# Smaller token tiles in a 32-expert layer: 96 rows for 128, a bias selector built per item, and the output scaling and the down bias moved

## What is computed

```
logits = h @ w_router + b_router                  # [512, 32]
top_vals, top_idx = top_k(logits, 4); gate = softmax(top_vals)
for each expert e, on the tokens that chose it:
    gu = x @ w_gate_up[e] + b_gate_up[e]          # 1024 -> 2048
    g, u = min(gu[:, :1024], 7), clip(gu[:, 1024:], -7, 7)
    y = ((u + 1) * g * sigmoid(1.702 * g)) @ w_down[e] + b_down[e]
    out[token] += gate * y
```

## Time and profile before

| what | value |
|---|---|
| median of 3 executions | 1663.77 us (1662.95 to 1666.04) |
| profiled execution, its own time | 1666.04 us |
| span in its profile | 1664.3 us |
| PE busy | 1597.3 us (96%) |
| DVE busy | 1310.5 us (79%) |
| ACT busy | 1074.0 us (65%) |
| moved | 476.58 MB, 286 GB/s |

### The profile page before, as it was taken

How to read it: one execution, slowest core, us unless ns; L and a number is a source line. 1 busy time by engine, 2 the same in 40 slices (tenths; PEclk the granted TensorE clock), 3 DMA queues, 4 the chain that set the end, 5 groups by cost and what they waited for, 6 DMA issues and landing times.

```text
span 1664.3 us, 21630 instructions
## 1 busy us (share of the span) xinstructions
PE 1597.3 (96%) x7527; PEld 1266.9 (76%) x7527; DVE 1310.5 (79%) x1016; ACT 1074.0 (65%) x1113; POOL 145.5 (9%) x113
## 2 busy tenths in 40 slices
PE   7999899999969999999999999999999999999993
PEld 6788555678858888888888888888888888888882
DVE  4465464545579999998999999899999889999973
ACT  5243343422367777777777777777777777777762
POOL 6500000000010000010000001000000100000010
PEclk9999899999979999999999999999999999999997
DMA  8332000004489999999999999999999999999973
GB/s 289 120 102 76 16 1 1 1 26 177 149 343 357 381 380 381 380 373 356 381 380 381 380 380 368 362 380 381 379 383 381 360 367 382 379 381 382 378 250 126
DMA packets 114382, 476.58 MB, mean 286 GB/s; under 512 B 9704, under 2 KB 10224, under 8 KB 97872
## 3 DMA queue, kind: packets, MB, share of 16 engines
q1 hardware_dynamic: 100528, 432.83, 68.1%
q0 software_dynamic: 10224, 37.62, 8.8%
q10 hardware_dynamic: 3600, 5.73, 1.0%
HBM read 451.24 MB, written 24.90 MB: 286 GB/s over the span
## 4 chain that ended last, share of the span: by engine, by line
PE 94%; DVE 3%; DMA 1%; ACT 1%; issue 0%; ACTq 0%; SPq 0%; DVEq 0%; POOLq 0%
PE ps L1174 26%; PE ps L1176 26%; PE ps L1175 26%; PE ps L1429 3%; PE ps L1269 2%; PE ps L1245 2%; PE ps L1401 2%; PE ps L1409 2%; PE ps L1282 2%; PE ps L1249 1%; PE ps L1289 1%; DVE mx L898 1%; DVE split L839 1%; PE ps L1353 0%; DMA xs<-in_x 0%
## 5 line engine op out<-in xcount | busy, mean ns | idle before, releaser
L1036 DVE TENSOR_TENSOR chunk_lo<-chunk,chunk_hi 128x2048 fp32r<-128x2048 f32 x384 | 861.7, 2284 | 56.7 <-ACT chunk_hi L660 54.0
L660 ACT ACTIVATE chunk_hi<-chunk 128x2048 fp32r<-128x2048 f32 x378 | 722.9, 1914 | 136.5 <-PE ps L1176 135.5
L1174 PE MATMUL ps<-chunk_hi,XT 128*128 128x512 f32 x1024 | 413.7, 404 | 2.0 <-DVE XT L1081 2.0
L1176 PE MATMUL ps<-chunk_hi,XT 128*128 128x512 f32 x1024 | 401.1, 392 | 0.0
L1175 PE MATMUL ps<-chunk_lo,XT 128*128 128x512 f32 x1024 | 400.5, 391 | 0.0
L1174 PEld LDWEIGHTS ps<-chunk_hi,XT 128*128 128x128 f32 x1024 | 193.7, 189 | 42.7 <-DVE XT L1081 2.4
L1176 PEld LDWEIGHTS ps<-chunk_hi,XT 128*128 128x128 f32 x1024 | 192.6, 188 | 40.8
L1175 PEld LDWEIGHTS ps<-chunk_lo,XT 128*128 128x128 f32 x1024 | 193.1, 189 | 37.7
L1174 PE MATMUL ps<-chunk_hi,hidT 128*128 128x512 f32 x512 | 205.4, 401 | 1.6 <-DVE hidT L1088 1.6
L1176 PE MATMUL ps<-chunk_hi,hidT 128*128 128x512 f32 x512 | 199.8, 390 | 0.0
L1175 PE MATMUL ps<-chunk_lo,hidT 128*128 128x512 f32 x512 | 199.6, 390 | 0.0
(11 more groups left out here) (235 smaller groups left out, 1890.5 us busy)
## 6 DMA issues: line engine op xcount, KB each, us to landing
chunk<-in_w_gate_up SPq DMA_DIRECT2D x256, 1024.0 KB, 8.9
chunk<-in_w_down SPq DMA_DIRECT2D x128, 1024.0 KB, 6.1
raw<-in_w_in SPq DMA_DIRECT2D x14, 1024.0 KB, 7.6
w_out<-in_w_out SPq DMA_DIRECT2D x4, 1024.0 KB, 5.9
xs<-in_x SPq DMA_DIRECT2D x4, 512.0 KB, 5.1
raw<-in_w_branch_a SPq DMA_DIRECT2D x2, 1024.0 KB, 5.1
raw<-in_w_branch_b SPq DMA_DIRECT2D x2, 1024.0 KB, 4.9
sum_rows<-xs ACTq DMA_DIRECT2D x4, 512.0 KB, 2.6
```

The costliest lines, as they stand in the source:

```text
L660: a.activation(chunk_hi[hi_slot(c, nxt)][:, :], chunk[c][:, :], ACT.Copy).then_inc(ex_hi, 1)
L1036: v.tensor_tensor(chunk_lo[c][:, :], chunk[c][:, :], chunk_hi[hi_slot(c, nxt, first)][:, :].bitcast(F32), ALU.subtract).then_inc(ex_lo, 1)
L1174: mm(dst, lhsT(0), rhs(0), start=start, stop=False)
L1176: return mm(dst, lhsT(1), rhs(0), start=False, stop=stop)
```

## The change

- `CAP` goes from 128 to 96: the stationary operands `XT`, `hidT` and `onehot` are 96 columns wide, 96 rows are gathered, transposed (8 matmuls of 96 rows x 128 stationary columns against a 96x96 identity) and added; outputs are 96 rows. The table for `npass` now allows up to 6 passes.
- The fixed `pick` gives way to `sel` (96x96 bf16), which DVE fills for each item (`choose_bias`: one tensor_scalar compare of `part_mod` with a column of `erow`). PE's `add_bias` uses 96 partitions and no register. DVE waits for `down_begun` before it overwrites `sel`; PE waits for `sel_ready`.
- The down bias moves from behind the gate bias of i+1 to right behind the up bias of i; PE's wait for `y_ready` moves with it. The index result moves to bank 6, and the wait for `f5_ready` moves ahead of `hidden_T`.
- `rows_out(i)` moves from behind the second chunk split of item i+1 to the end of item i, ahead of those splits.
- In the last item DVE makes `chunk_lo` 8 behind the two operations on `hid` and no longer ahead of them.
- The bias table loses its 32 rows of zeros.

```diff
-CAP = 128
+CAP = 96
-        part_mod = sb("part_mod", [128, E])
-        pick = sb("pick", [128, E], BF16)
+        part_mod = sb("part_mod", [128, CAP])
+        sel = sb("sel", [96, CAP], BF16)
-        idx_ps = ps[0:CAP, 5, 448:453]
+        idx_ps = ps[0:CAP, 6, 448:453]
@@ gpsimd
-            g.memset(bias_new[96:128, :], 0.0).then_inc(part_mod_set, 1)
-            pool.wait_ge(part_mod_set, 4)
...
-            pool.dma_start(bias_parts, bias_new[:, :]).then_inc(scattered, 16)
+            pool.dma_start(bias_parts, bias_new[0:96, :]).then_inc(scattered, 16)
@@ scalar
-            def act_item(i, nxt, before=True):
+            def act_item(i, nxt):
                 if nxt:
-                    ex_split_hi(i + 1, 0)
-                    ex_split_hi(i + 1, 1)
-                if before:
-                    rows_out(i - 1, 12 * i + 6)
-                if nxt:
-                    ex_split_hi(i + 1, 2)
+                    for c in range(3):
+                        ex_split_hi(i + 1, c)
                     rows_hi(i + 2, 0)
...
                     ex_split_hi(i + 1, 7)
+                act.wait_ge(gates_set, i + 3)
+                a.activation(gate_c[:, :], gates[:, bass.ds(i % 4, 1)], ACT.Copy).then_inc(gate_ready, 1)
+                act.wait_ge(ex_used, order(i, 11, nxt) + 3)
+                act.wait_ge(gate_ready, i + 1)
+                act.wait_ge(scattered, 16 * i + ADDED)
+                a.activation(ysb, ps[0:CAP, 4:6, :].rearrange("p t n -> p (t n)"), ACT.Copy,
+                             scale=gate_c[:, 0:1]).then_inc(y_ready, 1)
@@ vector
+            def choose_bias(e):
+                v.tensor_scalar(sel[:, :], part_mod[0:96, :], erow[0:96, bass.ds(e, 1)], None,
+                                ALU.is_equal).then_inc(sel_ready, 1)
...
                     ex_split_lo(i + 1, 3)
-                else:
-                    ex_split_lo(i, 8, nxt)
...
                 if nxt:
+                    dve.wait_ge(down_begun, i + 1)
+                    choose_bias((i + 1) % E)
                     rows_lo(i + 2, 1)
-                    ex_split_lo(i, 8, nxt)
+                ex_split_lo(i, 8, nxt)
                 ex_split_lo(i, 9, nxt)
@@ tensor
-            def add_bias(e, bank, part, start):
+            def add_bias(bank, part, start):
                 for t in range(2):
                     col = part * FF + t * 512
-                    last = mm(ps[0:CAP, bank + t, :], pick[:, bass.ds(e, 1)].to_broadcast([128, CAP]),
-                              bias_tab[:, col:col + 512], start=start, stop=not start)
+                    last = mm(ps[0:CAP, bank + t, :], sel[:, :], bias_tab[0:96, col:col + 512], start=start, stop=not start)
...
-                add_bias(i % E, 2, 1, False).then_inc(up_ps, 1)
+                pe.wait_ge(sel_ready, i + 1)
+                add_bias(2, 1, False).then_inc(up_ps, 1)
+                pe.wait_ge(y_ready, i + 1)
+                add_bias(4, 2, True).then_inc(down_begun, 1)
...
                         if c == 0:
-                            pe.wait_ge(y_ready, i + 1)
                             slots(i + 3)
                         if c == 1:
+                            pe.wait_ge(f5_ready, i + 4)
                             pe.wait_ge(xt_lo, 2 * i + 4)
                             hidden_T(i + 1)
-                    add_bias((i + 1) % E, 0, 0, False).then_inc(gate_ps, 1)
-                    pe.wait_ge(f5_ready, i + 4)
+                    pe.wait_ge(sel_ready, i + 2)
+                    add_bias(0, 0, False).then_inc(gate_ps, 1)
                 else:
                     hidden_T(i + 1)
-                    pe.wait_ge(y_ready, i + 1)
-                add_bias(i % E, 4, 2, True)
                 pe.wait_ge(hidT_lo, i + 1)
```

More of the change, by code:

```diff
@@ L134, in encoder_block @@
         ex = shared[:, 128:256].rearrange("p (c e) -> p c e", e=E)
-        onehot = shared[:, 256:512].bitcast(BF16).rearrange("p (c n) -> p c n", n=CAP)
+        onehot = shared[:, 256:448].bitcast(BF16).rearrange("p (c n) -> p c n", n=CAP)
         gains = sb("gains", [128, 2, HD])
@@ L194, in encoder_block @@
         part_mod_set = sem("part_mod_set")
-        pick_set = sem("pick_set")
         gcol_ps = sem("gcol_ps")
@@ L260, in encoder_block @@
         xt_lo = sem("xt_lo")
+        sel_ready = sem("sel_ready")
         gate_ps = sem("gate_ps")
@@ L272, in encoder_block @@
         hidT_lo = sem("hidT_lo")
+        down_begun = sem("down_begun")
         y_ready = sem("y_ready")
@@ L363, in _ @@
             sp.wait_ge(scattered, ADDED)
-            sp.dma_start(bias_tab[:, :], bias_parts).then_inc(bias_back, 16)
+            sp.dma_start(bias_tab[0:96, :], bias_parts).then_inc(bias_back, 16)
             sp.wait_ge(gathered, 16)
@@ L440, in _ @@
             for q in range(3):
-                g.iota(part_mod[32 * q:32 * q + 32, :], pattern=[[0, E]], base=0, channel_multiplier=1,
+                g.iota(part_mod[32 * q:32 * q + 32, :], pattern=[[0, CAP]], base=0, channel_multiplier=1,
                        allow_small_or_imprecise_dtypes=True).then_inc(part_mod_set, 1)
                 pool.wait_ge(part_mod_set, q + 1)
-            g.memset(bias_new[96:128, :], 0.0).then_inc(part_mod_set, 1)
-            pool.wait_ge(part_mod_set, 4)
             pool.wait_ge(zero_set, 1)
@@ L755, in _ @@
             act.sem_inc(y_ready, 1)
[L757 to L765, removed]
-            def act_item(i, nxt, before=True):
-                if nxt:
-                    ex_split_hi(i + 1, 0)
-                    ex_split_hi(i + 1, 1)
-                if before:
-                    rows_out(i - 1, 12 * i + 6)
-                if nxt:
-                    ex_split_hi(i + 1, 2)
+            def act_item(i, nxt):
+                if nxt:
+                    for c in range(3):
+                        ex_split_hi(i + 1, c)
                     rows_hi(i + 2, 0)
@@ L795, in act_item @@
                     ex_split_hi(i + 1, 7)
-            act_item(0, True, False)
-            with act.Fori(1, last_item) as i:
+                act.wait_ge(gates_set, i + 3)
[5 more added lines that the diff above has]
+                             scale=gate_c[:, 0:1]).then_inc(y_ready, 1)
+            with act.Fori(0, last_item) as i:
                 act_item(i, True)
             act_item(last_item, False)
-            rows_out(last_item, order(last_item, 11, False) + 3)
             a.activation(warm[:, :], eps[:, :], ACT.Sqrt)
@@ L1100, in _ @@
             serve(1)
+            choose_bias(0)
             for c in range(1, 3):
@@ L1441, in _ @@
             pe.wait_ge(bias_back, 16)
-            pe.wait_ge(pick_set, 1)
-            add_bias(0, 0, 0, False).then_inc(gate_ps, 1)
+            pe.wait_ge(sel_ready, 1)
+            add_bias(0, 0, False).then_inc(gate_ps, 1)
             pe.wait_ge(items_ready, 1)
@@ L1516 @@
     args.append(nc.dram_tensor("sum_rows", (SEQ + CAP, D), f32, kind="Internal").ap())
-    args.append(nc.dram_tensor("bias_parts", (128, 3 * D), mybir.dt.bfloat16, kind="Internal").ap())
+    args.append(nc.dram_tensor("bias_parts", (E * 3, 3 * D), mybir.dt.bfloat16, kind="Internal").ap())
     args.append(nc.dram_tensor("out", (1, SEQ, D), f32, kind="ExternalOutput").ap())
```

2 lines of the change are left out of this document (removed).

## The result

The changed kernel takes 1687.81 us (median of 4 executions, 1682.04 to 1690.54), where the kernel before takes 1664.28 in the same comparison: ratio 1.0136, 95% interval 1.0108 to 1.0165. It is 1.4% slower. The forecast was 1663.0, with 1647 to 1669 as its range.

The account below looks back on a forecast made before the run. PE's own pace was taken as the bound. Items sum to 0, first item -1.0, last +0.2: 1666.04 becomes 1665.2 for the profiled execution, 1663.0 against the median of 1663.77; range 1647 to 1669.

Parts of the forecast that it names:

- Narrower stationary operands: The 144 fp32r matmuls of an item: only the weight load shrinks, hidden under the matmul before; cost 0.
- rival A: The 13 ns each matmul has over its columns go with stationary width: -0.48 us an item, 1647 us; chance 0.13.
- Fewer POOL memsets at the start lie under the projections: Kernel start: POOL's saved memsets are covered by the projections; no time was put on them.
- First item: Split of rows and serve -0.15 x 3, smaller first gather -0.55; sum -1.0 us (-1.9 to -0.4).
- Last item: Hidden rows 0.9 us later, last scatter -0.7; sum +0.2 us; half clock, possibly 2 us, only named.
- Transposes: Transposes of rows in each item: the 128-column load holds, so 0; bounds -0.48 and 0, router matmuls' floor -0.19 us.
- Slots: Four onehot loads an item at 96 columns: +0.02 x 4 = +0.08 us, and -0.03 for the XT load behind.
- Moved steps: Off PE, the moved output scaling and choose_bias delay ACT and DVE, but idle gaps and cover absorb it; cost 0.
- B: Rival: transposes go with their moving columns, 96 for 128: -15.2 us, 1647 us in all; chance 0.08.
- C: Rival: slots' 96-column loads run at the four-byte rate: +0.14 to +0.22 us an item, 1668 to 1670; chance 0.07.
- D: Rival: ACT's new wait reaches PE through DVE in hidden_T, 0.3 us an item, 1672 us; chance 0.06.
- E: Rival: more passes, or something not thought of; no size given; chance 0.04.

Follow-up runs that it names:

- new_best: Changed kernel with XT, hidT, sel, onehot padded to 128 columns, the bias memset and old tail order back, DVE's first splits gated on POOL's first gather: 1667.77 us.
- new_rows_out_old: Changed kernel with the output scaling (rows_out) back behind ACT's second split of the next item: 1689.38 us, items 36.615 us.
- old_gate: Kernel before, with DVE's first three chunk splits waiting until POOL has issued the first gather: 1665.5 us, ratio 0.9997.

## Why the prediction was wrong

- **"Narrower stationary operands ... Cost 0"** is the step that failed. It bounded the 13 ns over the columns from below only (rival A) and held that a load hidden under a matmul can't cost; a loss was not priced at all. Measured: +0.397 us an item, 11.9 of the 22.4 us; width alone makes 0.30 of the 0.40 in the old kernel, the other 0.10 stays between layout and order. A covered load wasn't free to change: the pace of 0.2265 was that of one load length, and the trace of before has fp32r matmuls of 512 columns at no other width, so nothing bore the zero out. The Trainium skill, page TensorE: Matmul & The Clock Gate, section Back-to-back issue gap, says that the spacing in a stream is set by load and matmul together; the runs agree in so far as the spacing changes when the load does, and the direction they show, slower with a shorter one, is not in it.
- **"Fewer POOL memsets at the start lie under the projections"**: POOL's time is covered, but what DVE and PE meet there depends on when POOL runs. The stretch took 5.6 us more: 3.1 for the split held behind POOL, 1.6 for the half clock behind it, and 0.9 that stood before and is within what executions differ.
- **First item, -1.0**: +3.7 (4.4 at the gather, -0.7 behind). The smaller gather was priced by its bytes, and the POOL instruction ahead of it not at all, though the trace of before has 2.49 us for it, and about 1 in the items. That DVE holds this instruction is shown; what in the change makes it wait through four operations is open.
- **Last item, +0.2**: +2.6. The late hidden rows came as forecast (+0.9), the last scatter too (-0.6 for -0.7). The half clock, named at up to 2 us as a possibility and left out of the sum, took 1.5; the slower pace of the matmuls ahead of the pause (0.5) and behind it (0.2) the rest.
- **Transposes, 0 and at most -0.19 by the router's floor**: -0.06. Right.
- **Slots, +0.08, and -0.03 for the load behind**: +0.047 and -0.028, right in size. The start-to-start of the 96-column bf16 loads is 45 ns for 25; with 128 columns of `onehot` again (`new_best`) the slots are back at 24 ns each. The Trainium skill's page TensorE: Matmul & The Clock Gate (section on weight-path perf modes) has the fast load on at 128 columns only, and these rows agree; an estimate by the same page's P/1.2 ns (section LDWEIGHTS), 80 ns, is not reached here.
- **First load behind each block of transposes, -0.05**: -0.003. The gap of the first matmul there goes from 233.5 to 232 ns; a shorter load bought nothing.
- **Biases, 0**: -0.03. **Moved steps, 0**: 0, with the 3 us of idle DVE ahead of `chunk_lo` 0 that were forecast (3.40).
- **Rivals**: A and B did not come; C's slots cost what the forecast had for them and not C's 0.14 to 0.22; D was refuted by `new_rows_out_old`. What came falls under E, "something not thought of", with its chance of 0.04: A's term with the other sign, and three costs outside the items. No large error hid another: all of them went the same way.

## What to carry to other kernels

When PE's matmul stream is the bound, treat the stationary width as part of its pace and keep it at the width whose pace the trace shows; smaller tiles can be had by padding the operand with zero columns. Where a DVE operation reads two operands from SBUF while POOL reads SBUF, look at who issues first before removing or moving anything on either, however well it is covered, and let DVE wait for POOL where POOL's work is on the path. A pause of PE just ahead of the end is worth filling where the trace shows half clock behind it.

## What the runs showed of the hardware

- fp32r matmuls of 512 moving columns, end to end in a run: 227.0 to 227.9 ns with 128 stationary columns, 229.8 with 112, 230.2 to 230.9 with 96 and 230.4 with 64, though their loads last 189, 176, 162 and 137 ns.
- bf16 matmuls of 512 moving columns: 221, 217 and 255 ns with 128, 96 and 64 stationary columns.
- An indirect DMA's instruction on POOL, about 1 us in the items, took up to 8.11 while DVE subtracted two SBUF operands back to back, and ended 0.87 to 0.92 us behind the end of one of DVE's operations.
- The same DVE subtraction took 2.29, 3.51, 4.58, 7.68 or 8.18 us, by what POOL had begun before it.
- A pause of about 7 us in front of the down chunks was followed by full clock in one execution and by 14 matmuls at half clock in another of nearly the same kernel (`old_gate`).
